# Router logits and squares gathered inside a projection, and a recurrence that updates half of its columns

## The reference

```python
def rmsnorm(x, g):
    return x * lax.rsqrt(jnp.mean(x * x, axis=-1, keepdims=True) + EPS) * g

def hybrid_layer(...):
    ...
    x = x + jnp.einsum('bsd,de->bse', y, w_out)          # y: gated sum of two attentions
    h2 = rmsnorm(x, norm_ffn_g).reshape(b * s, d)
    return x + hierarchical_moe(h2, ...)

def hierarchical_moe(h, ...):
    group_logits = h @ w_router_group + b_router_group           # 8 groups
    p_group = softmax(group_logits); g_sel = argmax(group_logits)
    exp_logits = (h @ w_router_expert + b_router_expert)         # 32 experts, 4 in a group
    in_group = the 4 logits of group g_sel
    top_vals, top_idx = lax.top_k(in_group, 2)
    w_top = softmax(top_vals) * p_group[g_sel]
    out = sum over the two experts e: (silu(h @ w_gate[e]) * (h @ w_up[e])) @ w_down[e] * w_top

def rwkv7_recurrence(r, decay, k, v, a, b):       # 16 heads of 64 channels, 528 tokens
    # S_t = S_{t-1} diag(decay_t) + (S_{t-1} a_t) b_t^T + v_t k_t^T ;  y_t = S_t r_t
```

## Time and profile before

| what | value |
|---|---|
| median of 3 runs (lowest, highest) | 2410.09 us (2406.21, 2413.04) |
| the profiled execution: its time, its span | 2407.06 us, 2405.2 us |
| PE busy, PE weight loads busy | 2115.0 us (88%), 1801.0 us (75%) |
| DVE, ACT, POOL busy | 1331.7 us (55%), 942.0 us (39%), 742.1 us (31%) |
| matmul records | 19178 |
| DMA | 252.25 MB, 105 GB/s in the mean |
| granted clock of PE, mean | 0.925 of full speed |

### The profile page before, as it was taken

One profiled execution on the slowest core, in us unless ns is written; L12 is line 12 of the kernel. 1 busy time (PEld: TensorE's weight loads), 2 busy tenths in 40 slices (PEclk: granted clock), 3 DMA queues, 4 the chain that ended last, 5 costly groups with the idle time before them and its releaser, 6 DMA issues. The chain is left out here.

```text
span 2405.2 us, 45568 instructions
## 1 busy us (share of the span) xinstructions
PE 2115.0 (88%) x19178; PEld 1801.0 (75%) x19178; DVE 1331.7 (55%) x1881; ACT 942.0 (39%) x1468; POOL 742.1 (31%) x376
## 2 busy tenths in 40 slices
PE   7999998788799997799999787888888879999897
PEld 4777734466677776698999677777668879999685
DVE  2547635432688886405997675544542237787502
ACT  4214238621587886522223542222232233333312
POOL 2333300151112121143343263322033415555341
PEclk8998988788799998899999898999789999999899
DMA  4212210021699997123332011000122212322221
GB/s 166 88 62 70 70 53 1 18 82 41 253 357 351 349 363 282 46 88 116 93 128 79 27 67 44 5 4 4 38 89 71 76 39 89 96 88 92 67 96 44
DMA packets 68003, 252.25 MB, mean 105 GB/s; under 512 B 7664, under 2 KB 7664, under 8 KB 67056
## 3 DMA queue, kind: packets, MB, share of 16 engines
q1 hardware_dynamic: 65376, 240.70, 29.2%
q0 software_dynamic: 2448, 8.91, 1.0%
HBM read 234.18 MB, written 15.40 MB: 104 GB/s over the span
## 5 line engine op out<-in xcount | busy, mean ns | idle before, releaser
L1399 DVE TENSOR_TENSOR moe_wlo<-moe_ring,moe_whi 128x1024 fp32r<-128x1024 f32 x198 | 234.4, 1220 | 49.6 <-ACT moe_whi L1395 47.4
L504 PE MATMUL acc<-h_xhi,h_whi 128*128 128x264 f32 x816 | 235.4, 288 | 18.0 <-DVE h_xlo L444 12.2
L504 PE MATMUL acc<-h_xlo,h_whi 128*128 128x264 f32 x816 | 233.9, 287 | 0.0
L504 PE MATMUL acc<-h_xhi,h_wlo 128*128 128x264 f32 x816 | 233.8, 286 | 0.0
L1395 ACT ACTIVATE moe_whi<-moe_ring 128x1024 fp32r<-128x1024 f32 x198 | 205.0, 1059 | 56.5 <-DMA moe_ring<-moe_slabs 40.8
L504 PE MATMUL acc<-ff_xhi,ff_whi 128*128 128x258 f32 x704 | 201.4, 286 | 12.1 <-DVE ff_xlo L444 12.0
L504 PE MATMUL acc<-ff_xhi,ff_wlo 128*128 128x258 f32 x704 | 200.4, 285 | 0.0
L504 PE MATMUL acc<-ff_xlo,ff_whi 128*128 128x258 f32 x704 | 200.4, 285 | 0.0
L382 POOL TENSOR_TENSOR h_wlo<-ring,h_whi 128x1024 fp32r<-128x1024 f32 x51 | 122.4, 2402 | 194.0 <-ACT h_whi L377 194.0
L504 PEld LDWEIGHTS acc<-h_xhi,h_whi 128*128 128x128 f32 x816 | 156.3, 192 | 19.8 <-POOL h_wlo L382 16.3
L1831 DVE SCALAR_TENSOR_TENSOR acc<-cp,par,acc 128x528 f32<-128x528 f32 x232 | 159.2, 767 | 0.0
(11 more groups left out here) (484 smaller groups left out, 5569.1 us busy)
## 6 DMA issues: line engine op xcount, KB each, us to landing
ring<-slabs SPq DMA_DIRECT2D x213, 512.0 KB, 3.5
moe_ring<-moe_slabs SPq DMA_DIRECT2D x198, 512.0 KB, 5.3
tok_rows<-h_tok SPq DMA_DIRECT2D x5, 512.0 KB, 2.8
h_spill<-x SPq DMA_DIRECT2D x1, 2112.0 KB, 6.7
v_spill<-rw_v SPq DMA_DIRECT2D x1, 2112.0 KB, 7.4
y_spill<-cp SPq DMA_DIRECT2D x8, 264.0 KB, 4.5
rw_v<-v_spill SPq DMA_DIRECT2D x1, 2112.0 KB, 8.8
x<-h_spill SPq DMA_DIRECT2D x1, 2112.0 KB, 8.5
```

Source lines behind the costliest of these rows:

```text
L504: mm = nc.tensor.matmul(acc[j][0:rows, s, 0:t1 - t0], wp[:, at:at + rows], xp[:, t0:t1], start=(k == 0 and m == 0), stop=(k == kt - 1 and ...
L1399: tensor_tensor(wlo[u % AHEAD][:, :], ringm[u % AHEAD][:, :], whi[u % AHEAD][:, :].bitcast(F32), ALU.subtract).then_inc(w_lo[u % 2], 1)
```

## The change

- `normalize("ffn")` goes. In `out_projection` ACT makes, after each addition, `h` = `xt` x gain (without the root) and a square in one of four buffers. PE multiplies both inside the projection's block, two tiles late (`tally`): the router's 40 columns as weights with `h` as the moving side, summed over the eight parts in `acc[0][0:40, 1, :]`, and a 32-column matrix of 1/1024 with the square in `acc[1][64:96, 1, :]`. `tally(6)` and `tally(7)` follow the last tile.
- `route` loses its 64 matmul records of logits. POOL clears `lgt[96, 512]`, ACT and DVE copy the two sums into it, PE turns it with four transposes, ACT takes the root of the mean for each token (128x4), DVE the reciprocal, and the logits are product with it plus bias. `h_tok` is scaled by it in ACT's copy. Two small operations of ACT (`dummy`) call for the tables of the root and the exponential. The rank sums move to `acc[3]`.
- In the recurrence, `level_m` writes for M only the first block of 2^l columns of each pair of blocks, for MT only the second, 32 columns in place of 64, and DVE adds only these. DVE does M of both halves first and posts "m", then MT of both and posts "mt"; `level_x` waits for "m" alone.
- The four arrays of tile 0 are turned in its levels 1 to 4, where tiles 1 to 3 have their `back` pieces, and no longer in its tail.

```diff
-                normalize("ffn", lambda k: xt[:, k, :], lambda k: h[:, k, :], KD, T1, k0("mean1024"),
-                          lambda k: pcol("norm_ffn_g", k))
...
+                sq = [sbt(px, f"xo_sq{i}", [P, T1]) for i in range(4)]
...
+                    def tally(k):
+                        o = PCOL["router"] + 40 * k
+                        pe.wait_ge(gained, k + 1)
+                        nc.tensor.matmul(acc[0][0:40, 1, :], par[:, o:o + 40], h[:, k, :], start=(k == 0), stop=(k == KD - 1))
+                        pe.wait_ge(squared, k + 1)
+                        nc.tensor.matmul(acc[1][64:96, 1, :], k0("mean1024", 32), sq[k % 4][:, :], start=(k == 0),
+                                         stop=(k == KD - 1)).then_inc(tallied, 1)
+                    def behind(i):
+                        if i >= 2:
+                            tally(i - 2)
+                    pe_tiles(pe, w, "w_out", KD, KD, yx, T1, xo_ready, xo_out, then=behind)
+                    tally(6)
+                    tally(7)
...
-                    w.all_act(act, ["w_out"])
+                    def take(i):
+                        act.wait_ge(xo_out, i + 1)
+                        nc.scalar.activation(h[:, i, :], xt[:, i, :], ACT.Copy, scale=pcol("norm_ffn_g", i)).then_inc(gained, 1)
+                        if i >= 4:
+                            act.wait_ge(tallied, i - 3)
+                        nc.scalar.activation(sq[i % 4][:, :], xt[:, i, :], ACT.Square).then_inc(squared, 1)
+                    tile_loop(act, w, [("w_out", KD, 8)], take)
...
+                by_token = acc[2][:, 1, 0:384].rearrange("p (t n) -> p t n", t=4)
...
-                    sp.wait_ge(biased, 16)
...
+                    nc.gpsimd.memset(lgt[:, :], 0.0).then_inc(cleared, 1)
...
+                    pe.wait_ge(lgt_made, 2)
                     for tok in range(4):
-                        for k in range(KD):
-                            o = PCOL["router"] + 40 * k
-                            mm = nc.tensor.matmul(acc[tok][:, 0, 0:40], h[:, k, tok * P:(tok + 1) * P],
-                                                  par[:, o:o + 40], start=(k == 0), stop=(k == KD - 1))
-                        mm.then_inc(logits_ready, 1)
+                        mm = nc.tensor.transpose(by_token[:, tok, :], lgt[:, tok * P:(tok + 1) * P], k0("ident")[0:96, 0:96])
+                    mm.then_inc(lg_turned, 1)
                     for i in range(8):
                         if i >= 4:
                             pe.wait_ge(parted, i - 3)
                         tok, half = i // 2, i % 2
                         for q in range(4):
-                            mm = nc.tensor.transpose(acc[i % 4][:, 1, q * P:(q + 1) * P],
+                            mm = nc.tensor.transpose(acc[i % 4][:, 0, q * P:(q + 1) * P],
...
+                            nc.tensor.matmul(acc[3][:, 1, 8 * tok:8 * tok + 8], k1("before" if t == tok else "ones"),
...
+                    dve.wait_ge(cleared, 1)
+                    v.tensor_copy(lgt[64:96, :], acc[1][64:96, 1, :]).then_inc(lgt_made, 1)
+                    dve.wait_ge(rooted, 1)
+                    v.reciprocal(rstd[:, :], rstd[:, :]).then_inc(inverted, 1)
+                    dve.wait_ge(inverted, 1)
                     dve.wait_ge(biased, 16)
                     for tok in range(4):
-                        dve.wait_ge(logits_ready, tok + 1)
-                        L(v.tensor_tensor(lg[:, tok, :], acc[tok][:, 0, 0:40], rb[:, :], ALU.add))
+                        L(v.scalar_tensor_tensor(out=lg[:, tok, :], in0=by_token[:, tok, 0:40], scalar=rstd[:, tok:tok + 1],
+                                                 in1=rb[:, :], op0=ALU.mult, op1=ALU.add))
...
+                    act.wait_ge(cleared, 1)
+                    nc.scalar.activation(lgt[0:40, :], acc[0][0:40, 1, :], ACT.Copy).then_inc(lgt_made, 1)
+                    nc.scalar.activation(dummy[:, 0:1], k0("eps", 1, EPS_RMS), ACT.Sqrt)
+                    act.wait_ge(lg_turned, 1)
+                    nc.scalar.activation(rstd[:, :], by_token[:, :, 64], ACT.Sqrt, bias=k0("eps", 1, EPS_RMS)).then_inc(rooted, 1)
+                    nc.scalar.activation(dummy[:, 1:2], k0("eps", 1, EPS_RMS), ACT.Exp)
+                    act.wait_ge(inverted, 1)
                     for i in range(8):
                         act.wait_ge(turned, i + 1)
-                        nc.scalar.activation(h_tok[:, i // 2, i % 2 * 512:i % 2 * 512 + 512], acc[i % 4][:, 1, :],
-                                             ACT.Copy).then_inc(parted, 1)
+                        nc.scalar.activation(h_tok[:, i // 2, i % 2 * 512:i % 2 * 512 + 512], acc[i % 4][:, 0, :],
+                                             ACT.Copy, scale=rstd[:, i // 2:i // 2 + 1]).then_inc(parted, 1)
...
+                        if not ti:
+                            ev["pe"] += turned_early(l, "pe")
+                            ev["act"] += turned_early(l, "act")
                         ev["pe"] += [(ti, "m", u, l) for u in two]
-                        ev["dve"] += [(ti, "m", u, l) for u in two]
+                        ev["dve"] += [(ti, "m", u, l) for u in two] if l < nl - 1 else []
+                        ev["dve"] += [(ti, "mt", u, l) for u in two]
+                        if not ti:
+                            ev["dve"] += turned_early(l, "dve")
...
+            early = {1: TM_A, 2: TM_B, 3: TM_K, 4: TM_V}
...
+                firsts_of = lambda x, l: x.rearrange("p (b o t) -> p b o t", o=2, t=2 ** l)[:, :, 0, :]
+                seconds_of = lambda x, l: x.rearrange("p (b o t) -> p b o t", o=2, t=2 ** l)[:, :, 1, :]
...
-                            after(pe, "dve", ti, "m", u, l - 1)
+                            after(pe, "dve", ti, "mt", u, l - 1)
                         for q in range(8):
                             at = slice(q * CH, q * CH + tiles[ti][2][0][1])
                             if l < tiles[ti][3] - 1:
                                 for c, (c0_, cn) in enumerate(tiles[ti][2]):
-                                    mmul(bank(M_ + u)[part(1 - c, cn), at], MT[u][part(c, cn), q, 0:cn],
-                                         X[u][part(c, cn), q, 0:cn], start=True, stop=True)
+                                    mmul(firsts_of(bank(M_ + u)[part(1 - c, cn), at], l), MT[u][part(c, cn), q, 0:cn],
+                                         firsts_of(X[u][part(c, cn), q, 0:cn], l), start=True, stop=True)
                             for c, (c0_, cn) in enumerate(tiles[ti][2]):
-                                mm = mmul(bank(MT_ + u)[part(c, cn), at], X[u][part(c, cn), q, 0:cn],
-                                          MT[u][part(c, cn), q, 0:cn], start=True, stop=True)
+                                mm = mmul(seconds_of(bank(MT_ + u)[part(c, cn), at], l), X[u][part(c, cn), q, 0:cn],
+                                          seconds_of(MT[u][part(c, cn), q, 0:cn], l), start=True, stop=True)
...
+                    def turn_early(l):
+                        w = early[l]
+                        if w == TM_V:
+                            pe.wait_ge(v_back, 16)
+                        for g in two:
+                            if l > 1:
+                                after(pe, ("act", "dve")[g], 0, "tm", early[l - 1], g)
+                            turn(0, w, g, BACK + g)
...
+                                if l < nl - 1:
+                                    x = firsts_of(flat(M[u]), l)
+                                    did(tt(x, x, firsts_of(bank(M_ + u), l), ALU.add), "dve", ti, "m", u, l)
+                            for u in two:
                                 if l == 1:
                                     after(dve, "pool", ti, "mti", u)
-                                if l < nl - 1:
-                                    tt(M[u][:, :, :], M[u][:, :, :], eight(bank(M_ + u)), ALU.add)
-                                did(tt(MT[u][:, :, :], MT[u][:, :, :], eight(bank(MT_ + u)), ALU.add), "dve", ti, "m", u, l)
+                                x = seconds_of(flat(MT[u]), l)
+                                did(tt(x, x, seconds_of(bank(MT_ + u), l), ALU.add), "dve", ti, "mt", u, l)
...
```

More of the change, by code:

```diff
@@ L1260, in _ @@
                         for t in range(tok + 1):
-                            nc.tensor.matmul(acc[0][:, 0, 8 * tok:8 * tok + 8], k1("before" if t == tok else "ones"),
+                            nc.tensor.matmul(acc[3][:, 1, 8 * tok:8 * tok + 8], k1("before" if t == tok else "ones"),
                                              hot[:, t, :], start=(t == 0), stop=(t == tok))
                     for t in range(4):
-                        mm = nc.tensor.matmul(acc[0][:, 0, 32:40], k1("ones"), hot[:, t, :], start=(t == 0), stop=(t == 3))
+                        mm = nc.tensor.matmul(acc[3][:, 1, 32:40], k1("ones"), hot[:, t, :], start=(t == 0), stop=(t == 3))
                     mm.then_inc(ranked, 1)
@@ L2156, in counts, with turned_early @@
```

(63 more changed lines are left out.)

40 lines of the change are left out of this document (26 added, 14 removed).

## The result

The changed kernel takes 2396.74 us (median of 5 runs, 2393.57 to 2400.45) against 2410.09 (2406.21 to 2413.04): ratio 0.995, 95% interval 0.9931 to 0.997. That is faster, as forecast, by 0.5% where 0.9% was forecast. The median stands at the upper end of the range (2397), and the ratio gives 2398, beyond it.

A forecast was written before the change was run, and what follows sets the result against it. PE was taken as busy for 88% of the span, with instruction fetches pacing the recurrence. Gains of 14.9 + 6 = 20.9 us from 2407.06 gave 2386.2, put at a median of 2389 us, range 2374 to 2397.

The forecast's parts named there:

- Part one: Projection to experts: logits and squares tallied inside the projection let the experts start 14.9 us earlier.
- the tally: Projection: one tile's two matmuls, four records of 0.446 us, cost 1.78 us; all eight delay PE by 14.3 us.
- rival D: Dearer tallies, or route's chain waiting for POOL and ACT's table load: 5 to 15 us lost, 2396 to 2408; chance 0.06.
- no overlap of column groups: Projection: a tally's two matmuls priced in sequence at 14.3 us in all; side by side they would cost 8.8.
- the clearing: Route block: POOL's memset of 96x512, taken as 0.9 us.
- The wait for the exponential: Route block: DVE's wait of 1.11 us all but goes, as the exponential's table loads earlier.
- Part two: Recurrence: halved columns and M added first give 6 us, from 3 to 18, most DVE slack being retaken by instruction fetches.
- Tile 4: Recurrence's last tile, half the instructions: 1.6 us gained in each of two transitions, 3.2 us.
- I give tile 0 1.5 us and tiles 1 to 3 0.5 us each: Recurrence: the small gain left in these tiles, where the next instruction fetch takes back DVE's slack.
- Rival A: Recurrence: instruction feed does not bind, DVE's stalls go in every tile, 12 us more, 2377; chance 0.17.
- Rival B: Recurrence levels: PE's clock falls to its lower level, 36 us lost over 20 levels, 2431; chance 0.05.
- Rival C: Recurrence: strided columns slow the m matmuls; at 2.05 or 2.6 times their 0.78 us the gain is gone; chance 0.02.

The follow-up runs named there:

- place 0: Kernels whose recurrence lies where it does in TensorE's program of the kernel before; the old program there took 169.3, 170.1 and 169.4 us in tiles 1 to 3.
- old program: The recurrence code of the kernel before, also run in kernels with other parts changed or shifted; 272.2 us in the kernel before.
- new program: The recurrence code of the changed kernel, also run in kernels with other parts changed; 273.6 us in the changed kernel.
- part one alone: The changed kernel with the old recurrence: 2399.89 us, ratio 0.9947 to the kernel before.
- tiny_adds: The changed kernel with DVE's additions in tiles 1 to 3 cut to 128x32 (result no longer the layer): 2387.79 us in one run, 174.3 us in tiles 1 to 3.

## Why the prediction was wrong

**Part one** was right in mechanism and in its bound; the term that was mis-sized is the tally, 1.78 us taken from the mean's matmuls, 2.19 measured in the stream and 1.96 at the end. This is the direction of rival D, but not by its cause: the granted clock of the tallies was 1.00. Each matmul took 0.98 for two records, not 0.89, and 0.2 is lost where the stream resumes. From the first addition to PE's last sum it cost 16.8 us more than before (54.86 against 38.09), 14.5 forecast. That no overlap of column groups was taken was right: the rows show them in sequence. From PE's end to L1318's first run the sum had 4.65 us and the trace has 4.66 (the clearing 0.52 in place of 0.9, the root's table later). The wait for the exponential went, as forecast. 12.7 in place of 14.9.

**Part two** is where the larger error sits. The forecast said that the fetches take back DVE's gain in tiles 1 to 3, and they do: DVE's waits went, waits without a releaser came, and they end behind the fetches. But the 3 us still given to tiles 0 to 3 did not come, and tiles 1 to 3 at place 0 became 2.5 us longer (172.1 in one trace against a mean of 169.6 in three). Tile 4 gained 2 us (53.3 or so against 55.5 in five of seven traces of the old program, which has 53.8 and 58.3 in the others), 3.2 forecast. In all the new program takes 274.3 us in the mean of eight traces, the old one 274.1 at place 0 and 277.7 in the three others that have no pad inside: about nothing gained by itself, and 3.4 beside part one by the traces. The times can't confirm the 3.4: part one alone has a ratio of 0.9947, both parts have 0.995. The step that failed is "I give tile 0 1.5 us and tiles 1 to 3 0.5 us each": here the fetches left nothing of the slack, not even this part.

The sum then reads 12.7 + 0 in place of 14.9 + 6, and the ratio's 12 us agrees. The measured time lies where rival D had put it (2396 to 2408), but D named only tallies and the route's chain, and most of what is missing is in the recurrence. Rival A (no fetch bound, 12 us more) is excluded by the pauses that end behind landings and by tiny_adds. The rule that it went by, in the Trainium skill ("Runtime: NRT & Kernel Launch", section "Instruction fetch mechanics"), that crossing a block is "mostly hidden", does not fit this stretch, where 18 to 32 us in 170 are waits without a releaser. Rival B is excluded, the granted clock was 1.00 in tiles 1 to 3 of the changed kernel and 0.97 or more in the other new programs without a cut. Rival C too: an m of 64 records takes 0.92 to 0.96 us, before two of them took 1.92 (the 0.78 of the prediction was too low for both); the matmuls in strided columns show no cost that can be told, and PE was busy for 137.3 us where it was 140.1, with nearly the same records. So what rival C names from the Trainium skill ("Advanced Engine Details and Errata", section "PSUM Cachelines"), that non-contiguous patterns in PSUM slow matmuls, found no support in this kernel. A likely cause that no step had is the place of the program: part one moved the recurrence by 94 instructions, and where the old program was so moved it took some 3.6 us more (three traces against three, with the reserves above).

## What to carry to other kernels

Where an engine runs short instructions in thousands, count the instructions and look at the queue that brings them: where the engine's pauses end a fixed time behind its pulses, a shorter wait on another engine is worth nothing. An fp32 matmul with few weight columns took no less time than one with 128 (0.98 us against 0.89), so sums over channels that an idle DVE can add up first should reach TensorE once. After every step gained, look for the wait that was hidden behind it, here the DMA of 40 biases. And take the price of a matmul from a row that runs in the same company: small matmuls on two quarters of the array ran at half the rate of those on four.

## What the runs showed of the hardware

- All 27 pauses of TensorE over 0.8 us in three tiles ended 1.19 to 1.52 us after a block of 256 instructions had landed; the fetches started at least 3.3 and in the median 3.7 us apart.
- 64 instructions more in a level cost 0.95 us (14.2 us in 15 levels); the matmuls among them are 0.93 us of work by themselves.
- Fp32 matmuls of 64x64 weights that alternate between two quarters of the array start 0.029 us apart; over all four quarters 64 records took 0.92 to 0.96 us, 0.015 each.
- The same program took 169.3 to 170.1 us for three tiles at one place in TensorE's instruction stream (three traces) and 171.9 to 176.0 us at others (four traces); that the place does it is likely, not shown.
- Fp32 matmuls with 40 or 32 weight columns in different columns of the array ran one after the other, 0.98 us each for 512 columns, where those with 128 columns took 0.89.
